# 64x64 blocks in alternating quarters of the array for the recurrent tiles of a two-block transformer kernel

## Chip, cores and metric
One core of a Trainium2 chip. The time is the device time of one execution of the whole program, in microseconds (us). The kernel before ran three times: 4263.17, 4269.68 and 4270.6 us, median 4269.68.

## What is computed
The program is a two-block model on 256 latent tokens and 256 context tokens, width 1024. The change lies in one part of the first block, a recurrence with 4 heads of size 64, run forward and backward over the tokens, first over the context and then, from the state it left, over the latents:

```python
def step(S, inp):
    r_t, kk_t, v_t, w_t, b_t, k_t = inp
    sa = jnp.einsum('bhij,bhj->bhi', S, kk_t)
    S = S * w_t[:, :, None, :] - sa[..., None] * b_t[:, :, None, :] + v_t[..., None] * k_t[:, :, None, :]
    return S, jnp.einsum('bhij,bhj->bhi', S, r_t)
...
for d, reverse in enumerate((False, True)):
    ctx_state, y_c = wkv_scan(state0, *c_common, *c_dirs[d], reverse=reverse)
    _, y_l = wkv_scan(ctx_state, *l_common, *l_dirs[d], reverse=reverse)
```

The decay `w`, the vectors `b` and `k` and the direction `kk` are made from projections of the tokens. Beside the recurrence the mixer has a neighbourhood attention with 8 heads and a short convolution; an output projection, an expert layer with 16 experts per token and head, and a second block of four layers follow. Everything is in 32-bit floats.

## The kernel before
The program is a sequence of stages, each a block in which the five engines run their own instruction lists, with a barrier at its end. In order: modulation of the first block, norms and projections, `neighbour_stage` (attention, two heads per step, one on each half of the rows of the array for the scores and one on each half of its columns for the values), then `recurrent_mixer`, then the output projection, the expert layer and the second block.

`recurrent_mixer` (L2700) loads its constants, waits for them all, and calls `rw_tile_stage` for four tiles of 128 tokens (t = 0 and 1 are the context, t = 2 and 3 the latents), then `rw_chain_stage` and `rw_output_stage`. The recurrence is computed by chunks of 64 tokens, two chunks in a tile. Within a chunk it is solved with triangular matrices; across chunks `rw_chain_stage` multiplies 64x64 maps.

One call of `rw_tile_stage` (L2017), for both directions d:
- The front part. Two small products and two sums along the tokens (L2179 to L2189), a sigmoid and exponentials on ScalarE, and on VectorE the operands kc and bx of each direction (L2118 to L2128, the last in latent tiles only).
- L2201 transposes these per direction and head to 64 x 128, into the first 64 partitions of PSUM; L2083 copies them to chT, where direction d has partitions 64d to 64d+63. For direction 1 each transpose waits until the bank has been copied for direction 0.
- L2208 multiplies them to triangles, 128 x 128 per head, four kinds in latent tiles and two in context tiles. Both chunks stand in the one matrix, so it is block-diagonal after the mask of L2134.
- L2140 fills two matrices per direction with the identity. Then come the six levels (LEVELS = 6) of an inversion by doubling. In each, VectorE masks the triangle (L2151); TensorE forms Z (L2219, 4 heads of 128x128, for each direction); ScalarE copies Z (L2089); TensorE forms X, two products per head (L2226, L2228); VectorE subtracts them from the two matrices (L2150, twice). Z of both directions goes ahead of X of both. After the last level only one matrix is subtracted from (L2155).
- The tail: L2233 multiplies the triangle with v, L2240 applies the inverse, L2092 and L2096 copy; then for each direction L2248 to L2253 (latent tiles only) and, chunk by chunk, L2258, L2263 and L2264 with 64x64 operands. After each chunk TensorE waits for itself (`core.pe_steps.done`), and after both it tells VectorE, which moves psi, gamma, qT and y (L2163 to L2173).

In all of it the order on each engine is written out by hand, with semaphores counted up by one engine and awaited by another. SyncE issues no load during the tiles (`core.issue_w(sp, 0)`).

## Time and profile before
| | |
|---|---|
| median of three runs | 4269.68 us |
| the profiled execution | 4262.98 us, span 4260.9 us |
| TensorE matmul busy | 2950.2 us, 69% |
| VectorE busy | 2669.4 us, 63% |
| ScalarE busy | 1296.4 us, 30% |
| GpSimd busy | 729.5 us, 17% |
| moved by DMA | 860.28 MB, mean 202 GB/s |
| mean granted TensorE clock | 0.81 |

The profile names an instruction by its line, engine, operation and tiles. PE is TensorE's matmul, PEld its weight load, DVE VectorE, ACT ScalarE, SP SyncE. The granted clock of 1.0 stands for 2.4 GHz and 0.50 for 1.2 GHz. A duration of a matmul is that of its whole passage, in which several overlap; the pace of a series is read from the distance of the starts.

### The profile page before, as it was taken

The page shows a single profiled execution, that of the slowest core. Times are in us where ns is not written, and L with a number is a line of the kernel's source. Part 1 is how long each engine was busy: PE and PEld are TensorE (multiplying, and loading weights), DVE is VectorE, ACT ScalarE, POOL GpSimd, SP SyncE. Part 2 cuts the span into 40 slices and gives each one's busy share as a digit, 9 for nine tenths or more (in the row PEclk, how much of TensorE's full clock was granted, in tenths as well). Part 3 has the DMA queues.
Part 4 walks back from the last instruction along what each step waited for, and adds up shares of the span by engine and source line. Part 5 has one row for each costly group of instructions (what it writes and reads, how often), then busy time and mean ns, then how long its engine had stood idle before and what let it go on. Part 6 is the DMA issues. An engine that isn't in the chain of part 4 may idle for free. (4 is left out here: it accounts for less than half of the span.)

```text
span 4260.9 us, 51924 instructions
## 1 busy us (share of the span) xinstructions
PE 2950.2 (69%) x20092; PEld 2706.9 (64%) x20092; DVE 2669.4 (63%) x3946; ACT 1296.4 (30%) x1969; POOL 729.5 (17%) x566
## 2 busy tenths in 40 slices
PE   4956887700000000699689999799999799997899
PEld 3854777700000000699579999689898699996698
DVE  4635445188999998773448685467772686543454
ACT  1003221100000000334343434543434534342443
POOL 0000000105776776003000001300004000022000
PEclk9957888855555555899679999799999899996599
DMA  5950000307999999474119494267664194542043
GB/s 208 407 214 25 1 1 2 109 20 282 378 378 364 372 371 361 200 297 174 51 45 388 174 376 154 89 253 282 276 264 170 62 376 168 187 183 95 21 163 133
DMA packets 117943, 860.28 MB, mean 202 GB/s; under 512 B 14992, under 2 KB 16144, under 8 KB 17296
## 3 DMA queue, kind: packets, MB, share of 16 engines
q1 hardware_dynamic: 80624, 589.26, 35.8%
q0 software_dynamic: 36864, 268.45, 16.7%
q8 instruction: 114, 1.87, 0.2%
q14 instruction: 53, 0.43, 0.0%
q10 hardware_dynamic: 288, 0.26, 0.0%
HBM read 856.87 MB, written 1.05 MB: 201 GB/s over the span
## 5 line engine op out<-in xcount | busy, mean ns | idle before, releaser
L252 PE MATMUL ps<-h_hi,w_hi 128*128 128x256 f32 x3328 | 952.1, 286 | 37.9 <-DVE h_lo L533 16.4
L253 PE MATMUL ps<-h_lo,w_hi 128*128 128x256 f32 x3328 | 947.7, 285 | 0.0
L254 PE MATMUL ps<-h_hi,w_lo 128*128 128x256 f32 x3328 | 947.6, 285 | 0.0
L179 DVE TENSOR_TENSOR w_lo<-w_ring,w_hi 128x2048 fp32r<-128x2048 f32 x284 | 649.7, 2291 | 472.4 <-ACT w_hi L174 470.6
L174 ACT ACTIVATE w_hi<-w_ring 128x2048 fp32r<-128x2048 f32 x330 | 629.8, 1914 | 682.6 <-PE ps L254 550.8
L252 PEld LDWEIGHTS ps<-h_hi,w_hi 128*128 128x128 f32 x3328 | 641.2, 193 | 51.4 <-issue 21.0
L253 PEld LDWEIGHTS ps<-h_lo,w_hi 128*128 128x128 f32 x3328 | 641.1, 193 | 3.2
L254 PEld LDWEIGHTS ps<-h_hi,w_lo 128*128 128x128 f32 x3328 | 641.0, 193 | 0.0
L179 POOL TENSOR_TENSOR w_lo<-w_ring,w_hi 128x2048 fp32r<-128x2048 f32 x46 | 212.2, 4631 | 2441.4 <-ACT w_hi L174 2441.4
L409 PE MATMUL ps<-identity,gate_cols 128*128 128x128 f32 x48 | 7.2, 323 | 857.8 <-PEq L3164 857.8
L409 PEld LDWEIGHTS ps<-identity,gate_cols 128*128 128x128 f32 x48 | 7.0, 236 | 857.9 <-issue 857.9
L2945 POOL DMA_INDIRECT expert_rows<-in_experts,expert_col x256 | 379.0, 1481 | 212.8 <-POOL expert_col L2941 206.0
L238 DVE SCALAR_TENSOR_TENSOR mod_acc<-a_ring,cond,mod_acc 128x2304 f32<-128x2304 f32 (+1 forms) x138 | 353.6, 2588 | 50.8 <-DMA a_ring<-in_a_stream 23.4
L2991 DVE SCALAR_TENSOR_TENSOR expert_sum<-expert_rows,expert_coef,expert_sum 128x1024 f32<-128x1024 f32 x256 | 328.9, 1285 | 9.7 <-DVE expert_coef L2988 0.3
L2976 DVE CUSTOM_DVE_ANT_0 expert_junk<-expert_rows,h 128x1024 f32<-128x1024 f32 x256 | 306.8, 1225 | 44.1 <-DVE expert_sum L2991 21.5
L254 PE MATMUL ps<-w_hi,hid_lo 128*128 128x512 f32 x704 | 277.0, 393 | 0.0
L253 PE MATMUL ps<-w_lo,hid_hi 128*128 128x512 f32 x704 | 275.1, 391 | 0.0
L252 PE MATMUL ps<-w_hi,hid_hi 128*128 128x512 f32 x704 | 275.0, 391 | 0.0
L2964 ACT ACTIVATE expert_coef<-expert_dot 128x2 f32<-128x2 f32 x128 | 26.0, 203 | 657.3 <-DVE expert_dot L2976 657.3
L252 PE MATMUL ps<-w_hi,h_hi 128*128 128x256 f32 x544 | 159.4, 293 | 19.1 <-POOL w_lo L179 9.6
L2941 POOL COPY expert_col<-expert_idx 128x1 uint32 (+1 forms) x256 | 124.8, 487 | 218.4 <-SPq L2926 215.1
L253 PE MATMUL ps<-w_lo,h_hi 128*128 128x256 f32 x544 | 158.3, 291 | 0.0
(451 smaller groups left out, 4919.3 us busy)
## 6 DMA issues: line engine op xcount, KB each, us to landing
w_ring<-in_w_stream SPq DMA_DIRECT2D x360, 1024.0 KB, 4.8
a_ring<-in_a_stream SPq DMA_DIRECT2D x128, 1152.0 KB, 11.3
a_ring<-in_m_stream SPq DMA_DIRECT2D x24, 1024.0 KB, 9.2
mod_acc<-in_mod_start SPq DMA_DIRECT2D x6, 2304.0 KB, 9.0
alibi<-in_alibi SPq DMA_DIRECT2D x3, 2048.0 KB, 8.7
expert_rows<-in_experts,expert_col POOLq DMA_INDIRECT x256, 6.2
a_ring<-in_norm_post_row SPq DMA_DIRECT2D x3, 1024.0 KB, 4.5
na_bias<-in_na_bias SPq DMA_DIRECT2D x1, 2048.0 KB, 7.7
```

The costliest lines, as they stand in the source:

```text
L174: act.activation(self.w_halves(n)[0], self.w_item(n), ACT.Copy).then_inc(self.hi_made, 1)
L179: pool.tensor_tensor(self.w_halves(n)[1], self.w_item(n), self.w_halves(n)[0], ALU.subtract).then_inc(self.lo_made, 1)
L238: last = dve.scalar_tensor_tensor(out=acc, in0=item, scalar=cond, in1=acc, op0=ALU.mult, op1=ALU.add)
L252: pe.matmul(out, stationary[0], moving[0], start=start, stop=False)
L253: pe.matmul(out, stationary[0], moving[1], start=False, stop=False)
L254: return pe.matmul(out, stationary[1], moving[0], start=False, stop=stop)
L409: last = pe.matmul(core.ps[:, 1 + 2 * s + half, j * P:(j + 1) * P], bass.AP(col.tensor, col.offset, [list(col.ap[0]), [0, P]]), core.ident ...
L2941: core.pool_steps.done(pool, pool.tensor_copy(col[:, slot:slot + 1], idx[:, t, n]))
L2945: pool.indirect_dma_start(rows[:, slot, :], None, core.io["experts"], bass.IndirectOffsetOnAxis(ap=col[:, slot:slot + 1], axis=0)).then_in ...
L2964: act.activation(coef[:, b, :], dot[:, b, :], ACT.Gelu_apprx_tanh).then_inc(acts.sem, 1)
L2976: ins = dve.tensor_tensor_reduce(junk[:, e, :], rows[:, slot, 0:D], core.h2[:, t, :], 1.0, 0.0, ALU.mult, ALU.add, dot[:, b % G_BATCHES, e ...
L2991: dve.scalar_tensor_tensor(out=acc[:, t, :], in0=rows[:, slot, D:2 * D], scalar=c[:, e:e + 1], in1=acc[:, t, :], op0=ALU.mult, op1=ALU.add ...
```

## The change
Only the recurrent tiles and their constants are touched. What was kept as a 128x128 block-diagonal matrix is now kept as two 64x64 blocks, one above the other on the partitions: block c on partitions 64c to 64c+63. `tri` and the matrices of the levels have 64 columns per head in place of 128, and a product takes two matmuls, one in the quarter of the array with rows and columns of chunk 0 and one in that of chunk 1.
- The transposes take both directions at once, 128 x 128 per head, and so wait for both directions' operands.
- The triangles are four 64x64 matmuls per head and kind, in the order of quarters (0,0), (1,1), (0,1), (1,0), where the row is the direction and the column the chunk. Two kinds share a bank and one masking instruction.
- Level 0 starts from the identity: its Z is one product with `eye`, and VectorE forms both matrices from it. There are no identity copies and no X.
- In levels 1 to 4 X puts both its products in one bank and VectorE subtracts them in one instruction. Level 5 computes only the product that is used. The masks of the next level go ahead of the subtractions on VectorE.
- The product with v (L2233 before) goes between level 0 and level 1, on banks of its own.
- The maps alternate the chunks for every head; the self-waits go.
- Semaphores are per direction, and TensorE waits twice ahead of each Z.
- The masks have 64 columns, the matrices of the sums are a constant of their own (`rw_cums`), and `rw_eye` is new: seven loads in place of five.

```diff
+            def by_chunk(dst, stationary, moving, done):
+
+                for h in range(RW_H):
+                    for c in range(2):
+                        ch = slice(c * CHUNK, (c + 1) * CHUNK)
+                        last = pe.matmul(dst(h)[ch], stationary(h)[ch], moving(h)[ch], start=True, stop=True)
+                        if done is not None and h == RW_H - 1:
+                            last.then_inc(done.sem, 1)
...
+            pe.wait_ge(s["nats"].sem, s["nats"].at(2))
+            for i in range(n_ch):
+                for h in range(RW_H):
+                    src = kc[:, 0, h, :, :] if i == 0 else bx[:, i - 1, h, :, :]
+                    last = pe.transpose(core.ps[:, 4 + i, h * P:(h + 1) * P], src.rearrange("p d n -> p (d n)"),
+                                        core.ident[:])
+                last.then_inc(s["turn1"].sem, 1)
+            for g in range(groups):
+
+                pe.wait_ge(s["turn1_out"].sem, s["turn1_out"].at(3 + g))
+                for i in (2 * g, 2 * g + 1):
                     src, dst = ((1, 0), (2, 0), (1, 3), (2, 3))[i]
                     for h in range(RW_H):
-                        last = pe.matmul(core.ps[:, 4 * d + i, h * P:(h + 1) * P], chT[part(d), src, h, :],
-                                         chT[part(d), dst, h, :], start=True, stop=True)
-                    last.then_inc(s["tri"].sem, 1)
-            for level in range(LEVELS):
+                        at = (i % 2) * RW_W + h * DH
+                        for d, c in ((0, 0), (1, 1), (0, 1), (1, 0)):
+                            ch = slice(c * CHUNK, (c + 1) * CHUNK)
+                            last = pe.matmul(core.ps[ch, 2 * d + g, at:at + DH], chT[part(d), src, h, ch],
+                                             chT[part(d), dst, h, ch], start=True, stop=True)
...
+            for d in range(2):
+                pe.wait_ge(w["lvl_in"][d].sem, w["lvl_in"][d].at(1))
+
+                pe.wait_ge(w["tri_out"][d].sem, w["tri_out"][d].at(groups))
+                by_chunk(columns(4 * d, 0), matrix(d, 3), lambda h: rw.eye, w["lvl_z"][d])
+            for d in range(2):
+                by_chunk(columns(6 + d, 0), lambda h: tri[:, d, 1, h, :], lambda h: a.v[:, t, hd(h)], w["cv"][d])
+            for level in range(1, LEVELS):
                 for d in range(2):
...
+                    pe.wait_ge(w["lvl_new"][d].sem, w["lvl_new"][d].at(level))
+                    pe.wait_ge(w["lvl_in"][d].sem, w["lvl_in"][d].at(level + 1))
+                    by_chunk(columns(4 * d, 0), matrix(d, 3), matrix(d, 0), w["lvl_z"][d])
                 for d in range(2):
...
+                    pe.wait_ge(w["lvl_z_out"][d].sem, w["lvl_z_out"][d].at(level))
+                    if level + 1 < LEVELS:
+                        by_chunk(columns(4 * d + 1, 0), matrix(d, 1), matrix(d, 2), None)
+                    by_chunk(columns(4 * d + 1, RW_W), matrix(d, 2), matrix(d, 1), w["lvl_x"][d])
```

VectorE's side of the levels:

```diff
+            for d in range(2):
+
+                dve.wait_ge(w["lvl_in"][d].sem, w["lvl_in"][d].at(1))
+                dve.wait_ge(w["lvl_z"][d].sem, w["lvl_z"][d].at(2))
+                dve.tensor_tensor(lvl(d, 1), spread(rw.eye[:], RW_H), lvl(d, 3), ALU.subtract)
+                steps.done(dve, dve.tensor_tensor(lvl(d, 0), spread(rw.eye[:], RW_H), half(4 * d, 0), ALU.subtract))
+                dve.sem_inc(w["lvl_new"][d].sem, 1)
+                dve.tensor_tensor(lvl(d, 3), tri[:, d, 0, :, :], spread(rw.masks[:, d, 3, :], RW_H),
+                                  ALU.mult).then_inc(w["lvl_in"][d].sem, 1)
+            for level in range(1, LEVELS):
+                if level + 1 < LEVELS:
+                    for d in range(2):
+                        dve.wait_ge(w["lvl_z"][d].sem, w["lvl_z"][d].at(2 * level + 2))
+                        dve.tensor_tensor(lvl(d, 3), tri[:, d, 0, :, :], spread(rw.masks[:, d, 3 + level, :], RW_H),
+                                          ALU.mult).then_inc(w["lvl_in"][d].sem, 1)
                 for d in range(2):
...
+                    dve.wait_ge(w["lvl_x"][d].sem, w["lvl_x"][d].at(2 * level))
+                    if level + 1 < LEVELS:
+                        both = late[:, d, 0:2 * RW_W]
+                        dve.tensor_tensor(both, both, core.ps[:, 4 * d + 1, :], ALU.subtract).then_inc(
+                            w["lvl_new"][d].sem, 1)
```

## Rows read from the trace of the kernel before

**Rows 1.** The page, 40 equal slices of the span: what the DMA engines moved.
```profile
GB/s 208 407 214 25 1 1 2 109 20 282 378 378 364 372 371 361 200 297 174 51 45 388 174 376 154 89 253 282 276 264 170 62 376 168 187 183 95 21 163 133
```

**Rows 2.** Stretches: length, busy us (records) of each engine, granted clock, DMA share, GB/s.
```profile
377.00:453.00 76.00, 63.62 (x506) 57.45 (x506) 36.26 (x71) 19.91 (x37) 0.00 (x0) 0.86 0.00 1
...
529.00:617.00 88.00, 74.57 (x594) 67.81 (x593) 41.46 (x81) 20.71 (x39) 0.00 (x0) 0.87 0.00 1
...
704.00:723.00 19.00, 17.88 (x176) 16.37 (x176) 13.29 (x32) 0.00 (x0) 0.00 (x0) 0.50 0.01 2
```

**Rows 3.** Timeline, one level on TensorE: start us, length us, engine, line, operation.
```profile
564.38 1.16 PE L2219 MATMUL ps<-early 128*128 128x128 f32 x8 [0.19 <-DVE early L2151]
...
567.17 0.39 PE L2226 MATMUL ps<-early 128*128 128x128 f32 x2
...
570.52 0.39 PE L2228 MATMUL ps<-early 128*128 128x128 f32 x2
571.11 1.16 PE L2219 MATMUL ps<-early 128*128 128x128 f32 x8 [0.20 <-DVE early L2151]
```

**Rows 4.** Timeline of VectorE: last operand ahead of the transposes, and one level.
```profile
542.21 0.42 DVE L2128 TENSOR_TENSOR early<-early,r 128x256 f32<-128x256 f32 x1
...
569.16 1.29 DVE L2150 TENSOR_TENSOR early<-early,ps 128x512 f32<-128x512 f32 x2 [3.04 <-PE ps L2228]
...
570.97 1.28 DVE L2150 TENSOR_TENSOR early<-early,ps 128x512 f32<-128x512 f32 x2
```

**Rows 5.** Timeline, tail of a context tile: pairs of 64x64 records, one quarter throughout.
```profile
520.62 0.28 PE L2263 MATMUL ps<-v,bx 64*64 64x64 f32 x2
...
521.44 0.28 PE L2264 MATMUL ps<-mg,bx 64*64 64x64 f32 x2
```

**Rows 6.** Timeline: first Z of the first tile; then the first latent tile's front.
```profile
398.78 1.62 PE L2219 MATMUL ps<-early 128*128 128x128 f32 x6 [2.94 <-DVE early L2151]
...
539.77 1.03 PE L2201 MATMUL ps<-identity,kc 128*64 128x128 f32 x4 [1.37 <-DVE early L2128]
...
545.74 7.07 PE L2208 MATMUL ps<-chT 64*128 64x128 f32 x64
555.75 3.75 PE L2219 MATMUL ps<-early 128*128 128x128 f32 x16 [2.94 <-DVE early L2151]
```

**Rows 7.** Timeline, end of the chain stage on TensorE.
```profile
718.32 0.31 PE L2302 MATMUL ps<-state,psi 64*64 64x64 f32 x1
718.38 0.31 PE L2310 MATMUL ps<-state,rw_qT 64*64 64x64 f32 x1
718.42 0.31 PE L2302 MATMUL ps<-state,psi 64*64 64x64 f32 x1
...
718.59 4.14 PE L2310 MATMUL ps<-state,rw_qT 64*64 64x64 f32 x61
```

**Rows 8.** Timeline, neighbourhood attention: values with column halves in turn, then transposes.
```profile
346.29 1.09 PE L2639 MATMUL ps<-probs_T,na_v 128*64 128x128 f32 x16
347.32 1.09 PE L2624 MATMUL ps<-identity,logits 128*128 128x128 f32 x8
```

**Rows 9.** Timeline, tail of the first latent tile and the next tile's first product.
```profile
599.37 2.00 PE L2240 MATMUL ps<-kc,early 128*128 128x128 f32 x16
601.31 1.09 PE L2248 MATMUL ps<-tri,mg 128*64 128x128 f32 x8
...
607.68 1.06 PE L2248 MATMUL ps<-tri,mg 128*64 128x128 f32 x8
...
616.86 1.66 PE L2179 MATMUL ps<-rw_up,waT 64*128 64x256 f32 x6 [2.99 <-PEq L2025]
```

**Rows 10.** Groups by line, the four tiles (377 to 704 us): busy us, mean ns of one.
```profile
L2163 DVE TENSOR_TENSOR psi<-ps,identity 64x256 f32<-64x256 f32 x16 | 6.7, 418 | 42.7 <-PEq L2266 42.7
...
L2118 DVE TENSOR_TENSOR kc<-early,kk 128x256 f32<-128x256 f32 x8 | 3.4, 426 | 16.8 <-ACT p_end L2076 16.8
...
L2092 ACT ACTIVATE kc<-ps 128x256 f32<-128x256 f32 x8 | 3.1, 384 | 17.3 <-PE ps L2233 17.3
```

More of the change, by code:

```diff
@@ L2159, in _ @@
+            for d in range(2):
+                dve.wait_ge(w["maps"][d].sem, w["maps"][d].at(2))
                 for c in range(2):
@@ L2243, in _ @@
-            for d in range(2):
-                pe.wait_ge(s["mg_out"].sem, s["mg_out"].at(d + 1))
+                        at = (i % 2) * RW_W + h * DH
[3 more added lines that the diff above has]
+                                             chT[part(d), dst, h, ch], start=True, stop=True)
+                            if i % 2 and h == RW_H - 1:
+                                last.then_inc(w["tri"][d].sem, 1)
@@ new lines, in _ @@
+                    for h in range(RW_H):
+                        for c in range(2):
+                            ch = slice(c * CHUNK, (c + 1) * CHUNK)
+                            pe.matmul(core.ps[ch, 4 * d + 3, hd(h)], tri[ch, d, 3, h, :], a.v[ch, t, hd(h)],
+                                      start=True, stop=False)
+                        for c in range(2):
+                            ch = slice(c * CHUNK, (c + 1) * CHUNK)
+                            pe.matmul(core.ps[ch, 4 * d + 3, hd(h)], tri[ch, d, 2, h, :], mg[ch, d, h, DH:P],
+                                      start=False, stop=True)
@@ L2268, in rw_tile_stage @@
+                    for c in range(2):
+                        ch = slice(c * CHUNK, (c + 1) * CHUNK)
+                        dst = core.ps[part(d), 4 * d + c, RW_W + h * DH:RW_W + (h + 1) * DH]
+                        last = pe.matmul(dst, bx[ch, 0, h, d, :], mg[ch, d, h, DH:P], start=False, stop=True)
+                        if h == RW_H - 1:
+                            last.then_inc(w["maps"][d].sem, 1)
     for n in ("kk_root", "kk_sum"):
         s[n].passed(1)
-    for n in ("wa_up", "wa_in", "wa_out", "cums", "p_ready", "nats", "cv", "cv_out", "mg", "mg_out", "maps",
-              "lvl_x_out"):
+    for n in ("wa_up", "wa_in", "wa_out", "cums", "p_ready", "nats"):
@@ L2272, in rw_tile_stage @@
         s[n].passed(2)
     for n in ("turn1", "turn1_out"):
-        s[n].passed(2 * n_ch)
-    for n in ("tri", "tri_out"):
-        s[n].passed(8 if is_x else 4)
-    for n in ("lvl_in", "lvl_z", "lvl_z_out", "lvl_x"):
-        s[n].passed(2 * LEVELS)
+        s[n].passed(n_ch)
+    for d in range(2):
+        for n, count in (("tri", 2 * groups), ("tri_out", groups), ("lvl_in", LEVELS), ("lvl_z", 2 * LEVELS),
+                         ("lvl_z_out", LEVELS - 1), ("lvl_x", 2 * LEVELS - 2), ("lvl_new", LEVELS), ("cv", 2),
+                         ("cv_out", 1), ("mg", 2), ("mg_out", 1), ("maps", 2)):
+            w[n][d].passed(count)
```

218 lines of the change are left out of this document (95 added, 123 removed).

## Prediction
> **What bounds the kernel now.** I first read the slices of the page: in the 8% of the span that the change touches, some 377 to 704 us, the memory queues move next to nothing [rows 1], so no transfer can be uncovered there. Then the busy time by tile: two context tiles of 76.0 us, two latent tiles of 88.0 us (the second 87), and a chain stage of 19 us behind them [rows 2]. Each tile is a block of its own with a barrier at its end, so each microsecond that a tile loses is one of the kernel. TensorE is busy for 84% of a tile, VectorE for half. So I read one level in order of time. TensorE: a group Z of 8 records for each direction (a 32-bit matmul shows as two records), then X for both, 32 records, one per 0.112 us ((570.52 − 567.17)/30). The next level begins 6.73 us after this one (571.11 − 564.38) [rows 3]. VectorE: per direction two subtractions of 512 columns, 1.29 us together, and a mask, 1.81 us until the next direction's turn (570.97 − 569.16), begun 0.3 us after the X that they read [rows 4]. The loop closes as latency 0.3, VectorE 1.8 + 1.9, Z of direction 1 0.9, X of direction 0 1.8, sum 6.7. So both engines stand in it, and halving one alone would not halve the level.
>
> **The tile in three parts.** Latent tile: 27.1 us to the first Z (555.75, the block begins at 528.7), 43.6 us for six levels (599.37 − 555.75), 17.5 us for the tail (616.86 − 599.37) [rows 6, 9]. Context tile: 21.6 us to the first Z (398.78, the block begins at 377.2) [rows 6], the same 43.6, and the 10.8 us that are left of 76.0 [rows 2].
>
> **The unit of the new work.** A 64x64 block with 64 moving columns costs 0.0586 us a record when the same quarter is used again and again ((521.44 − 520.62)/14), at 2.4 GHz [rows 5]. Two such blocks in turn, 4 records, cost 0.23 us, as much as the 128x128 matmul that they replace (2 x 0.112). So on TensorE the change earns only what two quarters do at the same time. That they can is in the trace: at the end of the chain stage records of L2302 (rows and columns 64 to 127) and of L2310 (rows and columns 0 to 63) stand interleaved, each stream 0.10 us apart; this is the diagonal pair that `by_chunk` alternates. Then 61 records of L2310, in two column quarters of the same rows, take 4.14 us, 0.068 each, all of it at a granted clock of 0.50, which is 1.2 GHz [rows 2, 7]. At 2.4 GHz the nearest rows are the attention's, column halves alternating with 128 moving columns: 16 records until the next group 1.03 us later, 0.064 each, against 0.112 for a whole array [rows 3, 8]. No row shows two 64-column streams at 2.4 GHz. The bounds are 0.029, half of 0.0586, and 0.0586. I take 0.029: the steps at the ends of groups are in the means of both nearest rows, and without them each shows a factor near 2.
> The Trainium skill (TensorE: Matmul & The Clock Gate, Part 3, "The mechanism") says that matmuls in different tiles of the array run at once, but that a weight load overlaps only where the row group differs. The attention's column halves share their rows, and the trace shows them overlapping all the same; `by_chunk` differs in both, so the rule takes nothing from the sum.
>
> **The levels.** Matrices are 256 wide instead of 512. Z: 16 records, 0.47 us; X of a direction: 32, 0.93. VectorE subtracts both results in one instruction of 512 columns, 0.69 with its own run (two take 1.29 [rows 4]); the mask, 0.43 for 256 columns [rows 10], moves ahead of the wait for X and lies beside TensorE. ScalarE's copy of Z has 256 columns, 0.38 [rows 10]. From the end of X0 (X of direction 0): latency 0.3, subtraction 0.69, step to TensorE 0.14 (0.06 today [rows 3, 4]; doubled, as the added first wait stops the sequencer and nothing is fetched ahead), Z0 until 1.61. X1 ends at 0.93, its subtraction at 1.92, Z1 at 2.53; the copy of Z0 is ready at 2.3; X0 ends at 3.46. Period 3.5 us for 6.7, with TensorE and VectorE in the loop as before. Level 0 has no X: Z0, latency, two subtractions and a mask of 0.43, the same for direction 1, Z and X of level 1: X0 ends 4.1 us after the first Z at 2.4 GHz. Levels 2 to 4: 3 x 3.5. Level 5 computes half of X: 3.0, then 0.9 until the multiplication of L2240 begins. Sum 4.1 + 10.4 + 3.0 + 0.9 = 18.4. The start is cold today (L2219 x16 takes 3.75 us, 8 records later 1.16 [rows 3, 6]) and will be so for longer, as level 0 is thin: 2.5 us more if the clock rises after X of level 1, 9 if never; I take 4.1. So 22.5 for 43.6, −21.1 per tile, −84 for four.
>
> **The tail.** L2240: 16 records of 128 columns per direction, halved to 0.9. The maps alternate quarters and lose the waits between chunks: 48 records per direction in a context tile, 1.4 us; 96 in a latent one, 2.8 instead of 6.4 (607.68 − 601.31) [rows 9]. Chain: 0.9, latency and copy 0.9, maps of both, latency 0.3, VectorE's four evacuations, 0.42 each and overlapping to 0.34 [rows 10] (latent: also two for qT and one for y, 2.5), end 0.5. Context 6.7 for 10.8, latent 10.6 for 17.5.
>
> **Ahead of the levels.** Transposes pack both directions: 16 of 0.21 us (L2201: 4 in 1.03, the last one's own run in it [rows 6]) for 32 in a latent tile, 12 for 24 in a context one. But all wait for the second direction's operands (ready 14.0 us in, 542.21 + 0.42 − 528.7 [rows 4]; 13.6 in a context tile, which has no L2128), where direction 0's now lie beside VectorE. A triangle group becomes 64 records over four quarters, 3.4 us at 1.2 GHz, 1.9 at 2.4; today 64 full-width ones take 7.07 [rows 6]. Behind them latency, two masks of 0.69 and one of 0.43, overlapping, 2.1 us; today 2.9, with four identity copies. Context: 13.6 + 2.6 + copy 1.0 + 2.9 + 2.1 = 22.2 for 21.6. Latent: 14.0 + 3.4 + 0.2 + 4.5 (two groups, partly cold) + 2.1 = 24.2 for 27.1. The constants: the masks shrink from 10 KB per partition to 4, but two loads are added (2 KB and 0.25 KB); they end before the first tile and nothing covers them; −1 to +1 us, I take +0.5 for their issue. Strided writes of bx and kc: no row prices them, 0.43 for 256 columns stays [rows 10]; −0.1 to +0.3 us per tile. TensorE's sequencer passes two thirds more records in the levels (480 for 288 per tile); I cost that at nothing beyond F below.
>
> **The sum.** Context 22.2 + 22.5 + 6.7 = 51.4, −24.6. Latent 24.2 + 22.5 + 10.6 = 57.3, −30.9. Twice both −111, +0.5, so −110. The profiled execution took 4262.98 us (span 4260.9) and would take 4153. It lies 6.7 under the median of the three runs, at their low end; I add half of that: **4156 us**.
>
> **Rivals.** To price them I count TensorE's records in units of 64 moving columns: 760 in a context tile, 928 in a latent one. It waits besides for 20.0 and 21.4 us (operands 13.6 or 14.0, copy 1.0, masks 2.1, level 0 0.5, copy 0.8, end 2.0 or 3.0). If TensorE is the bound, a tile takes 760 F + 20.0 or 928 F + 21.4, which equals today's at F = 0.074 and 0.072.
> (a) The overlap works, but the clock stays at 1.2 GHz from the first Z on. For it: in the chain stage TensorE shows 17.88 of 19 us busy and is granted 0.50 throughout, overlapped quarters at its end included [rows 2, 7]. Against it: in today's tiles it rises within the first level [rows 3, 6]. F = 0.0535: 60.7 and 71.0, −65: 4201.
> (b) The pace stays at 0.0586 at 2.4 GHz, because array or instruction feed give no more; no record of this shape comes faster [rows 5]. 64.5 and 75.8, −48: 4218. What is left of the gain is VectorE's halves and the X that level 0 drops. The Trainium skill speaks for it (TensorEngine Tiling (Array Packing), "Instruction Overhead"): a matmul carries some 60 cycles of overhead, so no tiling factor should be taken from a dimension that is already small. The records of 0.0586 have 64 columns and follow each other without such an addition being visible.
> (c) Slower: the quarters don't overlap in `by_chunk` and the clock stays at 1.2 GHz, as in the single stream of L2302, which I count at 0.107 per record [rows 7]. It decides from 0.073 per record on. 101 and 121, +116: 4382. Against it is the interleaving itself.
> (d) No change, because something unseen holds the tile. Nothing in the trace speaks for it.
>
> **Chances.** Forecast 0.62 (own range 4132 to 4180: four quarters at once and an early high clock below, half of the overlap lost above), (a) 0.16, (b) 0.13, (c) 0.06, (d) 0.03. The range reaches over (a): 4132 to 4212. About 0.2%, 8.5 us, is what a measurement of this kernel can tell from no change. Faster: forecast, (a) and (b), 0.91; same 0.03; slower 0.06.
>
> **What would show it.** In the levels: two records per 0.058 us, period 3.5 us, clock 1.0 (forecast); 5.3 us at 0.50 (a); 5.8 us with TensorE without a gap (b); 10 us (c). The first Z 22.2 and 24.2 us into the tiles; tails of 6.7 and 10.6. I am wrong if anything past 704 us changes its length, or if the subtraction isn't what releases Z.

## The result and the profile after

The changed kernel takes 4129.7 us (median of four runs, 4125.5 to 4131.48) beside 4266.43 us for the kernel before, of which there are four runs now; the ratio is 0.9678, 95% interval 0.9661 to 0.9694. The profiled execution took 4131.48 us (span 4129.7), 131.5 less than that of before. The forecast was 4156 (profiled 4153) with a range of 4132 to 4212: right in direction and mechanism, 26 us too modest, and 2 us outside of its range.

Stretches, as in [rows 2] (length, busy us and records of PE, PEld, DVE, ACT, POOL, granted clock, DMA share, GB/s): the first context and the first latent tile, the chain stage, and then front and levels of the second and of the last tile.

```profile
379.00:425.00 46.00, 34.90 (x748) 30.65 (x748) 24.69 (x56) 14.83 (x31) 0.00 (x0) 0.78 0.01 2
...
472.50:524.50 52.00, 39.20 (x912) 35.51 (x912) 28.72 (x66) 15.41 (x32) 0.00 (x0) 0.80 0.01 2
...
576.00:594.00 18.00, 17.37 (x176) 16.09 (x176) 13.10 (x31) 0.00 (x0) 0.00 (x0) 0.53 0.01 2
...
425.10:450.50 25.40, 16.38 (x192) 13.65 (x194) 12.37 (x30) 9.80 (x19) 0.00 (x0) 0.53 0.01 2
451.00:470.00 19.00, 17.95 (x542) 17.06 (x538) 9.79 (x21) 4.65 (x11) 0.00 (x0) 1.00 0.01 3
524.70:542.50 17.80, 10.90 (x56) 8.43 (x60) 8.70 (x22) 9.16 (x18) 0.00 (x0) 0.53 0.00 1
543.00:575.00 32.00, 25.94 (x848) 24.62 (x836) 19.28 (x43) 5.80 (x14) 0.00 (x0) 1.00 0.01 3
```

The four tiles begin at 378.98, 425.10, 472.47 and 524.67 and take 46.1, 47.4, 52.2 and 51.0 us, 196.7 together, where they took 326.5: 129.8 of the 131.5 us lie there. TensorE's busy time in a tile falls to little more than half although it has half as many records again, and VectorE's by a third. The clock is near 1.2 GHz in a tile's front and 2.4 GHz in most of its levels: it rises to stay 18 to 26 us into the tile, where the first Z comes after 20 to 22.

The last tile on TensorE, whose levels lie wholly at 2.4 GHz; it starts at 524.67 (start us, length us; [rows 3, 6, 9] of before):

```profile
538.67 1.09 PE L2221 MATMUL ps<-identity,kc 128*128 128x128 f32 x4 [4.26 <-DVE bx L2135]
...
542.25 2.35 PE L2233 MATMUL ps<-chT 64*64 64x64 f32 x128
...
546.64 1.15 PE L2243 MATMUL ps<-rw_eye,early 64*64 64x64 f32 x32 [2.05 <-DVE early L2150]
...
548.93 0.68 PE L2243 MATMUL ps<-early 64*64 64x64 f32 x16 [0.21 <-DVE early L2159]
550.17 3.08 PE L2243 MATMUL ps<-early 64*64 64x64 f32 x96 [0.56 <-DVE early L2159]
553.51 3.11 PE L2243 MATMUL ps<-early 64*64 64x64 f32 x96 [0.25 <-DVE early L2171]
556.87 3.11 PE L2243 MATMUL ps<-early 64*64 64x64 f32 x96 [0.25 <-DVE early L2171]
...
565.38 1.96 PE L2243 MATMUL ps<-kc,early 64*64 64x128 f32 x32
```

A level takes 96 records and 3.36 us from start to start (556.87 − 553.51), for 6.73 before. The first Z of level 1 stands alone (x16 at 548.93), so a group of 96 begins with the Z of direction 1, goes on with both X and ends with the Z of direction 0 of the next level. Ahead of it TensorE is idle for 0.25 us, released by the subtraction of L2171 for direction 1. From the first Z (546.64) to the multiplication with kc (565.38) there are 18.74 us. Its tail lasts until 575.66, 10.3 us.

VectorE in the same levels: one subtraction of 512 columns per direction in place of two [rows 4] (first direction 0, then 1), and the masks (L2165) while TensorE works.

```profile
553.37 0.42 DVE L2165 TENSOR_TENSOR early<-tri,rw_masks 128x256 f32<-128x256 f32 x1
...
555.19 0.69 DVE L2171 TENSOR_TENSOR early<-early,ps 128x512 f32<-128x512 f32 x1 [0.51 <-PE ps L2243]
556.13 0.69 DVE L2171 TENSOR_TENSOR early<-early,ps 128x512 f32<-128x512 f32 x1 [0.25 <-PE ps L2243]
```

These rows close the loop through direction 1. Its Z, X of direction 0 and its own X are 80 records of 0.0294 us (the price measured below), 2.35 us. The subtraction of direction 1 begins 0.27 us behind them (556.13) and takes 0.69, and its next Z starts 0.05 us after that (556.87 − 556.82). The sum is 3.36. The Z of direction 0, 0.47 us, lies beside VectorE and costs nothing.

The subtraction over the four tiles:

```profile
L2171 DVE TENSOR_TENSOR early<-early,ps 128x512 f32<-128x512 f32 x32 | 22.0, 687 | 12.7 <-PE ps L2243 12.7
```

### The profile page after: what moved, and what is told of

Its sections match the earlier page's. It is cut to its first block and busy times, and to the rows that moved or that the text cites. A ratio compares the mean times of both kernels' runs of the same rounds, so it can differ in the third digit from the quotient of the medians.

```text
span 4129.7 us, 54148 instructions
## 1 busy us (share of the span) xinstructions
PE 2818.2 (68%) x21220; PEld 2587.5 (63%) x21220; DVE 2619.5 (63%) x3890; ACT 1275.5 (31%) x1947; POOL 724.0 (18%) x566
## 5 line engine op out<-in xcount | busy, mean ns | idle before, releaser
L252 PE MATMUL ps<-h_hi,w_hi 128*128 128x256 f32 x3328 | 953.3, 286 | 37.1 <-DVE h_lo L533 16.4
L252 PE MATMUL ps<-w_hi,h_hi 128*128 128x256 f32 x544 | 159.5, 293 | 19.3 <-POOL w_lo L179 9.6
L254 PE MATMUL ps<-w_hi,h_lo 128*128 128x256 f32 x544 | 158.1, 291 | 0.0
```

The lines of the kernel that those rows point to most:

```text
L252: pe.matmul(out, stationary[0], moving[0], start=start, stop=False)
L254: return pe.matmul(out, stationary[1], moving[0], start=False, stop=stop)
```

## The experiments

Each ratio is to the kernel before as it ran beside the experiment (medians of 4262.35 to 4266.51 us).

**The price of a record, measured by itself.** The changed kernel with a block ahead of the first tile that only issues matmuls of the identity; the 66 us that it adds are its own.

```diff
+            def one(r, c, i):
+                return (core.ps[at(c, 64), 6 + r, at(i % 8, 64)], core.ident[at(r, 64), at(c, 64)],
+                        core.ident[at(r, 64), 0:64])
...
+            for i in range(64):
+                pe.matmul(*one(0, i % 2, i), start=True, stop=True)
```

> The changed kernel with one block added ahead of the first recurrent tile that only measures: series of matmuls of 64x64 with 64 moving columns (two records each) on the identity, each series with its own pattern of quarters of the array: always (0,0); the diagonal pair in turn; two quarters in the same rows; two in the same columns; all four in turn; four matmuls in one quarter, then four in the other. First three of them cold, then 70 full-width matmuls, then all of them. Theory: every quarter is a server of its own, 0.0586 us a record at 2.4 GHz, and records of different quarters run at once whatever rows or columns they share: 0.0293 us per record for each of the three pairs, 0.0147 for all four, 0.0586 for one; double of each at 1.2 GHz. Rival, array or feed limits: all four no faster than a pair, 0.029. Rival, shared rows: the pair in the same rows near 0.0586, the diagonal pair and the pair in the same columns 0.029. For four and four: 0.0586 if a record waits in line behind its neighbour of the same quarter (less one overlap at each turn), 0.029 if records further back in line may pass. In sentences apart: the Trainium skill (TensorE: Matmul & The Clock Gate, Part 3, The mechanism) says that a weight load overlaps only where the row group differs, by which the pair in the same rows would pay its loads in full. TensorEngine Tiling (Array Packing), Instruction Overhead, gives each matmul some 60 cycles of overhead, by which four quarters would not come down to 0.0147.

The series on TensorE, a line of code each. L2762, L2769: one quarter; L2772: diagonal pair; L2775: same rows; L2778: same columns; L2766: all four; L2784: four and four. The clock rises from 1.2 to 2.4 GHz ahead of L2766.

```profile
377.91 10.36 PE L2762 MATMUL ps<-identity 64*64 64x64 f32 x95 [10.01 <-PEq L2793]
...
392.80 3.04 PE L2766 MATMUL ps<-identity 64*64 64x64 f32 x189
...
411.60 3.94 PE L2769 MATMUL ps<-identity 64*64 64x64 f32 x64
...
416.56 3.95 PE L2772 MATMUL ps<-identity 64*64 64x64 f32 x128
...
421.52 3.95 PE L2775 MATMUL ps<-identity 64*64 64x64 f32 x128
...
426.49 3.95 PE L2778 MATMUL ps<-identity 64*64 64x64 f32 x128
...
438.27 4.99 PE L2784 MATMUL ps<-identity 64*64 64x64 f32 x128
```

In the time of 64 records of one quarter any pair of quarters does 128: 0.059 us a record for one, 0.0294 for each of the three pairs between first and last start. All four: 0.0153 (L2766, 192 records between starts at 392.70 and 395.62). One quarter at 1.2 GHz (L2762): 0.107. Every quarter behaves as a server of its own: four at once lose some 4% (0.0153 for a quarter of 0.059), and what a quarter shares with another doesn't matter. The rival of the shared rows falls: L2775 is as fast as L2772. In a sentence apart: the Trainium skill (TensorE: Matmul & The Clock Gate, Part 3, "The mechanism") lets a weight load overlap with running matmuls only where the row group differs; here two quarters of the same rows lose nothing (0.0294), and the measurement decides. Four and four came to 0.0376 (L2784), between the two theories.

**Orders and widths.** The same block with other series.

```diff
+            for i in range(64):
+                pe.matmul(*one(i // 8 % 2, i // 8 % 2, i), start=True, stop=True)
...
+            for i in range(32):
+                pe.matmul(core.ps[:, 5, at(i % 8, 64)], core.ident[:], core.ident[:, 0:64], start=True, stop=True)
```

> The changed kernel with a measuring block ahead of the first recurrent tile, after 110 full-width matmuls so that the clock is 2.4 GHz: two, three, eight and sixteen matmuls in quarter (0,0), then as many in (1,1); 400 matmuls over all four quarters; then 32 moving columns and 64 moving columns through the whole array, 32 through one quarter, and 32 through the diagonal pair. Four and four gave 0.0376 us a record, between the 0.0294 of strict alternation and the 0.0591 of one quarter. If the array takes a few matmuls ahead of their turn: two and two 0.029, three and three near it, eight and eight some 0.048, sixteen and sixteen 0.053. Widths, if the time of a record goes by its columns alone: whole array 0.056 for 64 and 0.028 for 32, one quarter 0.029 for 32 columns, pair 0.0147. Rival, a fixed part: 32 columns take clearly more than half of 64. 400 matmuls over four quarters: 0.0153 throughout, or gaps of the kind seen once in the last series (1.5 us in which TensorE waited for nothing that the profile shows) if its instructions come no faster. In a sentence apart: the Trainium skill (TensorEngine Tiling (Array Packing), Instruction Overhead) gives a matmul some 60 cycles beside its columns, by which 32 columns would cost nearly what 64 do.

L2763, L2769, L2772: two, eight, sixteen in turn; L2775: 400 over all four; L2778, L2781: whole array, 64 and 32 moving columns; L2784: one quarter, 32 columns.

```profile
407.34 3.06 PE L2763 MATMUL ps<-identity 64*64 64x64 f32 x96
...
415.62 6.42 PE L2769 MATMUL ps<-identity 64*64 64x64 f32 x128
...
423.06 7.14 PE L2772 MATMUL ps<-identity 64*64 64x64 f32 x128
...
435.93 2.10 PE L2775 MATMUL ps<-identity 64*64 64x64 f32 x128 [1.00 <-issue]
439.39 2.09 PE L2775 MATMUL ps<-identity 64*64 64x64 f32 x128 [1.37 <-issue]
...
452.28 7.26 PE L2778 MATMUL ps<-identity 128*128 128x64 f32 x64
...
460.32 10.97 PE L2781 MATMUL ps<-identity 128*128 128x32 f32 x64
...
473.09 13.86 PE L2784 MATMUL ps<-identity 64*64 64x32 f32 x128
```

The orders, two, three (96 records in 2.97 us), eight and sixteen: 0.030, 0.031, 0.049 and 0.055 us a record. The single starts within these series say how far the array looks ahead. With three, four, eight and sixteen alike, the first record of the other quarter starts when three records of the quarter in use are still to come: the 30th record of L2772 starts 6 ns behind the 29th, where the first quarter has 32. So a record for a free quarter passes up to three that wait for a busy one, one and a half matmuls, and that covers a whole turn only where it is two or three matmuls long. The widths came out against me: 64 moving columns through the whole array take 0.111 a record, as much as 128, and 32 take 0.112 while the clock is 2.4 GHz and 0.213 after it has fallen at 463.3; in one quarter at 1.2 GHz 32 columns take 0.107, as 64 did (and 0.053 in the diagonal pair). The time of a record has a floor: 0.111 for the whole array, 0.059 for a quarter. That it goes with the columns of the stationary operand and not with its rows, a row of the changed kernel says, all 128 rows and 64 columns, with two moving columns, at 1.2 GHz:

```profile
431.82 1.01 PE L2209 MATMUL ps<-chunk_sum,early 128*64 128x2 f32 x8
```

Its records start 0.107 us apart, as those of a quarter do; the whole array takes 0.213 at this clock. Each record of all these series loads its stationary operand anew; whether it is the load that sets the floor wasn't tested.

In a sentence apart: the Trainium skill (TensorEngine Tiling (Array Packing), "Instruction Overhead") has a fixed overhead of some 60 cycles as floor; a floor is there, but it halves with the columns of the stationary operand.

And 400 matmuls in a row over four quarters don't keep their pace: after the first 236 records 1.0 us of "issue" follows, and then 1.4 to 1.6 us behind each 128, a mean of 0.025 a record (a gap of 1.5 us stands in the first block's series over four quarters too). I read this as instructions that come no faster; no run tests it.

**The order within a level.** by_chunk takes four heads of chunk 0, then four of chunk 1.

```diff
-                for h in range(RW_H):
-                    for c in range(2):
+                for c in range(2):
+                    for h in range(RW_H):
```

> The changed kernel, but by_chunk takes the four heads of one chunk one after the other and then those of the other chunk, where it alternated; the same records, only their order differs. Theory A, only neighbours in line overlap: 0.0586 us a record in the levels, as the second price of the forecast had it (F), so Z 0.94 instead of 0.47, X of a direction 1.9 instead of 0.93, period 5.6 to 5.8 instead of 3.36, levels to the multiplication with kc some 30 us instead of 19.4, the multiplication and tails a little more: +11 to +12 us per tile, about 4130 + 46 = 4176. That would be the whole gain that comes from the alternation. Theory B, the array lets later records of a free quarter pass: 4130 and period 3.36, and the order in the code is worth nothing; then only the quarters themselves count.

Measured: 4139.44 us, ratio 0.9702 (0.9685 to 0.9718), tiles together 210.7. A level takes 4.04 us:

```profile
456.57 3.85 PE L2243 MATMUL ps<-early 64*64 64x64 f32 x96 [0.19 <-DVE early L2171]
460.61 3.85 PE L2243 MATMUL ps<-early 64*64 64x64 f32 x96 [0.19 <-DVE early L2171]
```

Neither theory: the starts of the 96 records are 0.038 us apart, the pace of the measured series four and four. Alternating is worth 0.7 us a level, 12 to 14 us in the tiles and about 10 in the kernel's time; most of the overlap would come without it.

**Every block twice**, to give TensorE the pace of the second rival.

> The changed kernel, but by_chunk issues every 64x64 matmul twice, with the same result in the same place. Per 64 columns of useful work TensorE then takes 0.0586 us instead of 0.0293 in the levels, the product with v and the multiplication with kc, which is the pace of the forecast's second rival (no two quarters at once). Asked: what that pace would have cost, and whether TensorE closes the loop. Theory, it does: 96 more records a level at 0.0293, so period 3.36 + 2.8 = 6.2 us; 576 more units in a tile, 16.9 us less what the product with v hides, some +16 a tile, 4130 + 64 = 4194, within a few us of the 4218 of that rival less the triangles and maps, which stay as they are here. Rival: latency and VectorE close the loop and TensorE has room: period 5.0 or below, 4165 or less.

```diff
+                        pe.matmul(dst(h)[ch], stationary(h)[ch], moving(h)[ch], start=True, stop=True)
                         last = pe.matmul(dst(h)[ch], stationary(h)[ch], moving(h)[ch], start=True, stop=True)
```

Measured: 4183.66 us, ratio 0.9811 (0.9796 to 0.9826), tiles together 250.4. VectorE's subtractions of direction 0 show the period:

```profile
474.95 0.69 DVE L2171 TENSOR_TENSOR early<-early,ps 128x512 f32<-128x512 f32 x1 [1.44 <-PE ps L2244]
476.82 0.69 DVE L2171 TENSOR_TENSOR early<-early,ps 128x512 f32<-128x512 f32 x1 [1.18 <-PE ps L2244]
...
480.67 0.69 DVE L2171 TENSOR_TENSOR early<-early,ps 128x512 f32<-128x512 f32 x1 [1.44 <-PE ps L2244]
```

5.72 us (480.67 − 474.95), that is 2.36 more for 2.8 us more of work. The loop of the rows above gives just this: of the 96 doubled records 80 lie in it, 2.35 us, and the 16 of the Z of direction 0 lie beside VectorE. So TensorE closes the loop together with VectorE's subtraction and two short steps, 1.0 us in both kernels. The second rival's 4218 also had transposes, triangles and maps at the slow pace, 2 × 184 + 2 × 352 units more, at 0.0293 up to 31 us: 4215. Its price was sound; its condition, no two quarters at once, is refuted by the first series.

**Less work, full width.** The kernel before, where level 0 has no X and no identity copies and level 5 computes only the used product.

```diff
+                    elif level == 1:
+                        dve.wait_ge(s["lvl_z"].sem, s["lvl_z"].at(d + 1))
+                        dve.tensor_tensor(lvl(d, 1), spread(core.ident[:], RW_H), lvl(d, 2), ALU.subtract)
+                        steps.done(dve, dve.tensor_tensor(lvl(d, 0), spread(core.ident[:], RW_H), bank(4 * d),
+                                                          ALU.subtract))
...
+                if level == 0:
+                    continue
...
+                        if level + 1 < LEVELS:
+                            pe.matmul(bank(4 * d + 1)[:, h, :], lvl(d, 1)[:, h, :], lvl(d, 2)[:, h, :],
+                                      start=True, stop=True)
```

> The kernel before with only the part of the change that drops work: level 0 forms both matrices from the identity without X and without the identity copies, and level 5 computes only the product that is used; everything stays 128x128 at full width. By the level's loop (latency 0.3, VectorE 1.8 and 1.9, Z 0.9, X 1.8): level 0 loses 2.8 us, level 5 about 1.8, the identity copies 0 to 1 us. That is 4.6 to 5.6 us a tile, -18 to -22 in all: 4244 to 4248 beside a before of 4266. Rival: the dropped work is most of the gain, since TensorE is the bound and level 0 and half of level 5 are a quarter of its records in the levels: then -60 or more, 4206.

Measured: 4225.41 us, ratio 0.9901 (0.9884 to 0.9917), twice what I expected and not the rival either. The second tile, first of the kernel before (it starts at 452.87), then of this one (444.30):

```profile
475.77 3.18 PE L2219 MATMUL ps<-early 128*128 128x128 f32 x16 [2.94 <-DVE early L2151]
...
483.18 1.16 PE L2219 MATMUL ps<-early 128*128 128x128 f32 x8 [0.19 <-DVE early L2151]
...
510.07 1.16 PE L2219 MATMUL ps<-early 128*128 128x128 f32 x8 [0.19 <-DVE early L2151]
...
518.18 2.00 PE L2240 MATMUL ps<-kc,early 128*128 128x128 f32 x16
```

```profile
464.79 2.84 PE L2220 MATMUL ps<-identity,early 128*128 128x128 f32 x16 [1.48 <-DVE early L2152]
468.03 1.70 PE L2220 MATMUL ps<-early 128*128 128x128 f32 x8 [0.40 <-DVE early L2152]
...
488.32 1.16 PE L2220 MATMUL ps<-early 128*128 128x128 f32 x8 [0.19 <-DVE early L2152]
...
495.04 1.16 PE L2220 MATMUL ps<-early 128*128 128x128 f32 x8 [0.19 <-DVE early L2152]
...
501.41 1.78 PE L2244 MATMUL ps<-kc,early 128*128 128x128 f32 x14
```

The period is untouched (495.04 − 488.32 = 6.72). In the kernel before the first Z of this tile is 22.90 us in, level 0 lasts 7.41 (475.77 to 483.18) and level 5 with the product with v 8.11 (510.07 to 518.18); here 20.49, 3.24 and 6.37. So level 0 was worth 4.2 us (booked 2.8; its first records ran at the low clock) and level 5 1.7 (1.8). The first Z comes 1.4 to 2.8 us earlier in the four tiles (booked 0 to 1): 1.5 us of it is the idle time ahead of Z, 2.94 and now 1.48, which the identity copies held; the rest lies ahead of that and goes with where the clock rose. The tiles take 294.7 us together, 31.8 less.

Of the 130 us that the change saves in the tiles, 32 need no quarters at all; 98 come with the blocks. The kernel with every block twice divides these: 54 (250.4 − 196.7) are what two quarters at once give in the levels, in the product with v and in the one with kc. The other 44 (294.7 − 250.4) come with the rest: one subtraction for two, the masks moved ahead (below), and shorter transposes, triangles and maps; no run takes them all apart.

**Triangles in pairs.**

```diff
-                        for d, c in ((0, 0), (1, 1), (0, 1), (1, 0)):
+                for pair in (((0, 0), (1, 1)), ((0, 1), (1, 0))):
...
+                            for d, c in pair:
```

> The changed kernel, but the triangles go through the array in two passes, first the quarters (0,0) and (1,1) in turn, then (0,1) and (1,0), where all four alternated. If four quarters at once is what made the triangle groups shorter than my forecast (0.94 us measured, 1.9 forecast at 2.4 GHz; 2.0 measured, 3.4 forecast at 1.2 GHz), a group of 64 records takes 1.9 us warm and 3.8 cold, the first Z comes 0.9 to 1.9 us later in each tile, and the kernel takes +4 to +8 us: 4134 to 4138. If the pace was set by something else (the chT copies on ScalarE, the masks on VectorE), the first Z stays where it is and so does the time, 4130.

Measured: 4130.23 us, ratio 0.9673 (0.9657 to 0.9689). The triangles of the first two tiles, first of the changed kernel (the first group at 2.4 GHz, the second at 1.2), then of this one (the first at 1.2, the second at 2.4):

```profile
396.13 1.16 PE L2233 MATMUL ps<-chT 64*64 64x64 f32 x64 [0.69 <-ACT chT L2093]
...
442.24 1.99 PE L2233 MATMUL ps<-chT 64*64 64x64 f32 x64 [0.69 <-ACT chT L2093]
```

```profile
395.99 3.32 PE L2234 MATMUL ps<-chT 64*64 64x64 f32 x64 [0.69 <-ACT chT L2093]
...
445.11 1.91 PE L2234 MATMUL ps<-chT 64*64 64x64 f32 x64 [0.69 <-ACT chT L2093]
```

The group takes 3.3 us at 1.2 GHz and 1.9 at 2.4, just what I had forecast for the change itself (3.4 and 1.9), where four quarters at once take 2.0 and 1.2. At the same clock that is worth 1.3 or 0.75 us a group. The first Z of the first tile comes 22.2 us in, again the forecast, but that agreement is in part luck: the changed kernel has 20.1 there with the clock risen before the triangles and 20.9 without (below). Over the four tiles the first Z comes 3.2 us later than in the changed kernel and is still 4.2 us earlier than forecast. In the kernel's time, 4134 to 4138 expected, nothing of it is seen: its tiles take 199.2 us together, for 196.7 and 198.6 in the changed kernel's two profiles, since the clock happened to rise earlier in the second tile.

**Masks behind the subtraction.**

```diff
+                        dve.tensor_tensor(both, both, core.ps[:, 4 * d + 1, :], ALU.subtract).then_inc(
+                            w["lvl_new"][d].sem, 1)
+                        dve.tensor_tensor(lvl(d, 3), tri[:, d, 0, :, :], spread(rw.masks[:, d, 3 + level, :], RW_H),
+                                          ALU.mult).then_inc(w["lvl_in"][d].sem, 1)
```

> The changed kernel, but VectorE masks the triangle for the next level behind the subtraction of each direction, as the kernel before does, and no longer ahead of the wait for X. By the loop of the levels: subtraction 0.69, mask 0.43, subtraction, mask in line, so Z of direction 0 starts some 0.4 us later and Z of direction 1 some 0.8 later, X of direction 0 behind it: period 3.9 to 4.0 us for 3.36, four such turns per tile, +2.2 us a tile, +9 in all: 4139. Rival: VectorE is not what closes the loop, as each direction has slack while TensorE works for the other: 3.4 us and 4130 to 4132.

Measured: 4140.0 us, ratio 0.9712 (0.9696 to 0.9728), tiles together 204.3; the period is 3.76 us and TensorE now waits for masks too:

```profile
461.14 0.68 PE L2240 MATMUL ps<-early 64*64 64x64 f32 x16 [0.28 <-DVE early L2168]
...
464.90 0.68 PE L2240 MATMUL ps<-early 64*64 64x64 f32 x16 [0.28 <-DVE early L2168]
```

The time is as expected, +10 us for +9; the period of 3.9 to 4.0 was too high, and the tiles have 6 to 8 us of it. VectorE stands in the loop too: the order of its two instructions is worth 0.4 us a level, beside 0.7 for the alternation of the quarters.

**One wait ahead of Z.** From level 2 on TensorE waits for the subtraction alone.

```diff
+                    if level == 1:
+                        pe.wait_ge(w["lvl_in"][d].sem, w["lvl_in"][d].at(level + 1))
```

> The changed kernel, but TensorE waits once ahead of each Z from level 2 on (for the subtraction alone, which VectorE issues behind the mask), as against twice. My forecast booked 0.14 us for the step from the subtraction to Z because of the second wait, 0.06 today. If that is right, the period falls from 3.36 to 3.28, some 1.1 us in all four tiles, to be seen only in the trace (idle ahead of Z 0.19 for 0.25). If the second wait is free, the period stays 3.36.

Measured: 4132.05 us, one run. The levels start 3.36 us apart with 0.25 idle, as with two waits, and Z starts 0.05 us after the subtraction in both. The second wait is free.

**Work that nothing uses, for the clock.** Nine transposes of the identity per tile in the gap ahead of the real ones; then five more in the gap ahead of the product with chunk_sum.

```diff
+            for i in range(9):
+                pe.transpose(core.ps[:, 6, (i % 4) * P:(i % 4 + 1) * P], core.ident[:], core.ident[:])
             pe.wait_ge(s["p_ready"].sem, s["p_ready"].at(2))
```

> The changed kernel with work added that nothing uses: 9 full-width transposes of the identity per tile, on TensorE while it waits for VectorE's operands, ahead of the real transposes (3.9 us at 1.2 GHz in a gap of 4.3). Asked: what the low clock costs at the start of the levels, for which I had booked 4.1 us a tile. If the clock rises earlier for it, transposes (2.9 us for 12 at 1.2 GHz), triangles (2.0 for 1.0) and the first levels (1.1) are what can shrink: 1 to 3 us a tile, 4118 to 4126. If the clock doesn't rise earlier: 4130, and the transposes start up to 0.2 us later. If TensorE is late for the operands: slower, 4132 to 4135.

> As the kernel with 9 idle transposes per tile, and 5 more ahead of the product with chunk_sum, in the gap of 2.2 us behind the first product of the tile. TensorE is then busy for nearly the whole front of a tile. If the low clock at the start of a tile comes from these gaps, the clock stays at 2.4 GHz or returns before the transposes: the cost of the low clock is then gone in full, 2.5 (transposes, triangles) + 1 (first levels) + 1.5 (the sums of L2213, 1.0 a piece warm for 2.07) a tile, 4110 to 4118. If only a part of it, between 4118 and 4130. If the extra work pulls the clock down later in the tile, 4130 and above.

Measured: 4132.49 us, ratio 0.9695 (0.9677 to 0.9711), and 4133.2 us, ratio 0.9693 (0.9677 to 0.9709). The second tile of the kernel with both:

```profile
434.29 1.72 PE L2219 MATMUL ps<-identity 128*128 128x128 f32 x9
...
441.49 1.98 PE L2237 MATMUL ps<-chT 64*64 64x64 f32 x64 [0.69 <-ACT chT L2093]
```

A transpose is one record of 0.19 to 0.21 us, not the two that I had counted, so the gaps were filled by half only. The clock went up for a moment and down again (435.4 to 438.9 in this tile; the triangles here run at 1.2 GHz). The tiles take 197.4 and 194.0 us together, for 196.7 and 198.6 in the two profiles of the changed kernel, and the kernel's time shows nothing of it. Whether a front without any gap would keep the clock at 2.4 GHz wasn't tried.

**Four quarters in the levels.** Since all four quarters run at once, Z's operands are kept in the other chunk's partitions, and the two products of X go through the two diagonals. Level 0 also forms both its matrices on TensorE, with one subtraction on VectorE for two instructions.

```diff
+                    z = (columns(4 * d, 0), matrix(d, 3), matrix(d, 0))
+                    by_quarters([z + (0, 1), z + (1, 0)], w["lvl_z"][d])
...
+                    own = (columns(4 * d + 2, 0), matrix(d, 2), matrix(d, 1))
+                    other = (columns(4 * d + 1, 0), matrix(d, 1), matrix(d, 2))
+                    crossed = [other + (0, 1), other + (1, 0)] if level + 1 < LEVELS else []
+                    by_quarters([own + (0, 0), own + (1, 1)] + crossed, w["lvl_x"][d])
```

> The changed kernel with all four quarters used in levels 1 to 4: the triangle of the levels and the matrix that Z reads lie in the other chunk's partitions, so that of the two products of X one goes through (0,0) and (1,1) and the other through (0,1) and (1,0), in two banks, and Z goes through (0,1) and (1,0). Level 0 forms both matrices on TensorE with all four and VectorE subtracts once. If any quarters run at once, as the series of the measuring block showed (0.0153 a record for four), X of a direction takes 0.47 us for 0.93. Loop of one direction: latency 0.3, subtraction 0.69, Z 0.47 and its step 0.25, ScalarE's copy 0.38 and its steps 0.5, X 0.47, sum 2.8 to 3.0 for 3.36: -0.4 to -0.5 us a level, -0.5 in level 0, some -2.3 a tile, 4120. If TensorE isn't what closes the loop, or the two banks cost VectorE more: 4130.

Measured: 4121.36 us (five runs, 4118.53 to 4126.05), ratio 0.9663 (0.9650 to 0.9676). Its levels:

```profile
449.47 2.48 PE L2244 MATMUL ps<-early 64*64 64x64 f32 x96 [0.37 <-DVE early L2172]
452.25 2.48 PE L2244 MATMUL ps<-early 64*64 64x64 f32 x96 [0.29 <-DVE early L2172]
```

2.78 us for 3.36, the tiles 186.2 us together for 196.7. 4120 was expected. Four such periods a tile are 9.3 us of the 10.5; the rest lies in level 0 and in where the clock rose.

**The changed kernel again.**

> The changed kernel as it is, again, for the spread of its tiles from one profiled execution to the next and as the mark for the kernel that uses all four quarters (4121.4, ratio 0.9663 to the kernel before). If the terms are as I now read them, every step between instructions repeats to 0.1 us and only the place where the clock rises differs: transposes 13.7 and 14.0 us into the tiles, first Z 20.0 to 20.9 (context) and 21.6 to 22.5 (latent), levels 18.7 to 19.9, tails 6.65 and 10.3 to 10.4, the four tiles together 194 to 198 us, the kernel 4126 to 4134. Rival: the first profile was a lucky one, and the cold start costs up to the 4.1 us a tile that I had booked: tiles together up to 209 us.

Measured: 4126.18 us (five runs, 4121.94 to 4136.31), ratio 0.9673 (0.9660 to 0.9686). Every step repeats to 0.1 us: transposes 13.67 and 14.0 us into the tiles, tails 6.64 and 10.3 to 10.4. The first Z comes at 20.9, 20.9, 22.5 and 22.2, the levels take 19.9, 20.1, 19.3 and 18.7, the tiles 198.6 us together, a little above what I expected. All nine runs of this kernel have a median of 4129.4, and the one with four quarters lies 8 us under it. The intervals of the ratios overlap, so the times alone don't settle it; the tiles' 10 to 12 us in the traces do.

## Why the prediction was right, and where it fell short

| step | forecast | measured (two profiles) |
|---|---|---|
| transposes start, context, latent | 13.6, 14.0 | 13.67, 14.0 |
| first Z, context | 22.2 | 20.1 to 20.9 |
| first Z, latent | 24.2 | 22.0 to 22.5 |
| pace of a record in the levels | 0.029 | 0.0294 |
| period of a level | 3.5 | 3.36 |
| levels, all at 2.4 GHz | 18.4 | 18.74 |
| added for the cold start, a tile | 4.1 | 0 to 1.3 |
| tail, context, latent | 6.7, 10.6 | 6.65, 10.3 to 10.4 |

The step that failed is the size of two terms of the sum, the cold start of the levels and the triangles; the mechanism held. The four tiles were forecast at 217.4 us and took 196.7. The missing 20.7 us are three terms:

- **The levels, 12.7 us, the largest.** The failed term is the cold start, "I take 4.1", a guess between 2.5 and 9 from the cold Z of [rows 3, 6]: 16.4 us in four tiles, of which the trace has 2.4. The other 1.4 go the other way, as the levels at 2.4 GHz take 18.74 for 18.4. The trace has one tile with its levels wholly at 2.4 GHz in each of the two profiles, 18.74 and 18.75 us, and the others, in which the clock rose up to 6 us after the first Z, at 19.3 to 20.1. In the second tile the clock is 1.2 GHz for the first 4.7 us of the levels. There Z of level 0 takes 1.97 us for 1.15 in the last tile and the product with v 1.92 for 1.10, but VectorE's three instructions per direction, which go on beside that product, take 0.41 to 0.43 us at either clock. All in all the tile's levels take 1.1 us more (19.8).
- **Ahead of the first Z, 7.4 us.** 6.5 of them are the triangles. I priced 64 records as two quarters at a time, 3.4 us cold and 1.9 warm, though the code alternates all four, and the kernel with the triangles in pairs shows these prices. Beside that kernel's groups at like clocks the quarters give some 4.6 us, 1.3 in each context tile and 1.0 in each latent one; the rest goes with where the clock rose and with the 4.5 booked for two groups, which take 3.4 to 3.7 even in pairs. The remaining 0.9 us are the copy and the masks of the context tiles, 0.69 us for 1.0 and 1.8 for 2.1.
- **The tails, 0.6 us**: right.

The gain was also counted from tiles a little too long: the sum takes 76.0 and 88.2 us twice, 328.4, where the four took 326.5.

Beyond the tiles, I had added 3.4 us for the place of the profiled execution within the runs of before; the changed kernel's median lies under its profiled execution instead. That the stages outside the tiles would keep their length holds: from the end of the last tile to the end of the program there are 3557.2 us before, and 3554.0 and 3557.4 in the two profiles of the changed kernel. The first tile starts 1.8 us later, but at 376.2 to 380.4 us in the executions of the kernels that share this code, so the constants' +0.5 can't be read.

Two reasons don't hold. The pace of 0.0586 I had put down to 64 moving columns; the widths show that the 64 columns of the stationary operand alone give it, and a quarter is cheap for that. The step of 0.14 us from the subtraction to Z, "as the added first wait stops the sequencer and nothing is fetched ahead", is 0.05 us in the trace, with two waits as with one; no run shows the 0.14, and its 0.09 too much are most of the difference between the period of 3.46 in the sum and 3.36.

Of the rivals, (a) fell where it mattered, as the clock was at 2.4 GHz from 18 to 26 us into each tile on; (b) and (c) fell by the measured series.

## What to carry to other kernels

Where matrices are block-diagonal or small, use every quarter of the array and let consecutive matmuls differ in their quarter: a record's time has a floor set by the columns of its stationary operand, and up to four quarters work at once, so that 64x64 blocks in series of up to some 200 records cost about a quarter of what they cost one by one. Then write the loop out, engine by engine, from one start to the next: here 2.35 us of TensorE and 1.01 of VectorE and steps, and only what lies in it pays. Price work at a low clock only for the part of a stretch that TensorE really closes. Before crediting a new layout, do the dropped work alone in the old one: here it was a quarter of the gain.

## What the runs showed of the hardware

- Quarters of the array run at once with next to no loss: 0.059 us a record for one, 0.0294 for two, whether they share rows, columns or nothing, 0.0153 for four (2.4 GHz).
- Records for a free quarter pass up to three waiting ones, one and a half matmuls: three and three in turn run at 0.031, four and four at 0.038, sixteen and sixteen at 0.055.
- 32 moving columns gain nothing over 64 in a quarter (0.107 both, at 1.2 GHz), and 64 or 32 nothing over 128 in the whole array (0.111 and 0.112).
- A series of 400 matmuls over four quarters falls into bursts: 128 records in 2.1 us, then 1.4 to 1.6 us of "issue".
- A second semaphore wait ahead of a group costs nothing that the trace shows.
